# Decays set two units ahead in the matrix memory, and negated maxima with scaled queries in attention

## The chip, the cores and the metric

The kernel runs on one core of a Trainium2 chip. The core has TensorE (PE), VectorE (DVE), ScalarE (ACT), GpSimd (POOL) and SyncE (SP), which issues most transfers. The metric is the device time of one execution in microseconds.

## What is computed

One batch of 256 latent and 256 context tokens of width 1024 goes through two blocks, all in float32. The first block has two layers, each a gated feed-forward part, a mixer of attention with a short convolution, and a second feed-forward part. The second block has a matrix memory ("mlstm") and a gated recurrence ("hgrn") beside each other, forwards and backwards, and a convolutional feed-forward part. The change touches the attention and the matrix memory:

```python
def attend(q, k, v):
    s = jnp.einsum('bqhd,bkhd->bhqk', q, k, preferred_element_type=jnp.float32) * ATTN_SCALE
    p = jax.nn.softmax(s, axis=-1).astype(v.dtype)
    return jnp.einsum('bhqk,bkhd->bqhd', p, v)

def step(carry, inp):                       # matrix memory, chunk by chunk
    C, n, m = carry
    qc, kc, vc, ic, fc = inp
    b = jnp.cumsum(fc, axis=-1)
    dlog = jnp.where(causal, b[..., :, None] - b[..., None, :] + ic[..., None, :], -jnp.inf)
    inter = b + m[..., None]
    mt = jnp.maximum(inter, jnp.max(dlog, axis=-1))
    w_intra = jnp.exp(dlog - mt[..., None])
    w_inter = jnp.exp(inter - mt)
    s = jnp.einsum('bhtd,bhsd->bhts', qc, kc) * w_intra
    num = jnp.einsum('bhts,bhsv->bhtv', s, vc) + w_inter[..., None] * jnp.einsum('bhtd,bhdv->bhtv', qc, C)
    den = jnp.sum(s, axis=-1) + w_inter * jnp.einsum('bhtd,bhd->bht', qc, n)
    h = num / jnp.maximum(jnp.abs(den), jnp.exp(-mt))[..., None]
    ...
```

## The kernel before

Each engine runs a program of its own, written out by hand, and the engines meet at counting semaphores. On each engine the order of work is the order in the code. `own.mark` counts an instruction of the same engine, and `own.wait` or `own.link` lets the engine wait for it. Weights stream from memory in units of 1 MB into a ring of slots (`raw`) that SyncE fills as slots come free. ACT rounds each half unit to a high part (L1094), DVE takes the remainder (L1565), and PE makes three products of high and low parts (L555, L563). That is most of the time.

**Attention.** After the projections ACT copies the queries of 8 heads out of PSUM (L1299) and DVE the keys. Then come units, each one head and 128 query rows: 32 in layer 0 (16 of them over 256 context keys, 16 over all 512 keys), 16 in layer 1 (512 keys). For unit n PE makes the scores (L852), DVE the row maximum (L1925, `small`) and its product with the negative scale (L1927), ACT the exponential with that as bias and the scale as factor, and its row sum (L1319), DVE the reciprocal (L1933) and the scaling (L1934). PE transposes the probabilities (L861) for unit n-2 of its loop, ACT copies them (L1328), PE multiplies them with the values for pairs of units (L874), and DVE splits the result into `h_hi` and `h_lo` (L1942, L1943). L1949 is a remainder of the convolution beside it. Three banks hold scores and two the transposes, so that three units are under way.

**Matrix memory.** It is computed in closed form, not chunk by chunk. There are 8 units: unit n is head n // 2 in direction d = n % 2. For each head PE makes the scores of 512 keys and 256 queries (`scores`, L997). For each unit PE spreads the row of running maxima over the partitions into bank 2 + d (`maxima`, L989). DVE adds the causal mask on two blocks (`mask`, L2145). ACT takes the exponentials, three with a bias from the bank (L1444) and two of the masked blocks (L1447); together they are `ml_decay[d]`. DVE weighs scores with them (`weigh`, L2158 and L2162), PE multiplies by the values (L1022), and `num_out` makes the rows: DVE the denominator and its reciprocal (L2186 to L2188), then for even units a scaled copy on ACT (L1474), for odd ones an addition on DVE (L2193) and sums of squares on ACT (L1482). Between these stand pieces of the other recurrence's output: a gate on DVE (`gated`, L2208), its rounding on ACT (`high`, L1489) and the remainder on DVE (`out_rest`, L2239). There are two buffers of decays and of weights, one for each direction. PE's loop over n waits for the weighing of unit n, then makes the maxima of unit n+2, then (odd n) the scores of the next head, then the products of unit n. ACT's loop takes the exponentials of unit n and then the rows of unit n-1. In the trace all these tiles are called `arena`, the PSUM banks `bank`, the maxima's operands `x` and `consts`, the causal mask `late`.

Of the kernel before, what the change touches and what calls it, by code (L numbers as in the profile page):

```python
# [27 lines left out]
ACT = mybir.ActivationFunctionType  # L28
ALU = mybir.AluOpType
AX_X = mybir.AxisListType.X  # L30
# [151 lines left out]
def build_program(nc, stream, columns_in, cond_in, x_in, ctx2_in, params_in, consts_in, out, until=None):  # L182
    with ExitStack() as stack:
# [326 lines left out]
        def _(pe):  # L510
# [455 lines left out]
            def mlstm():  # L966
# [43 lines left out]
                for n in range(2 * MH):  # L1010
                    hd, d = n // 2, n % 2
                    pe.wait_ge(sem("ml_weighted"), n + 1)
                    if n + 2 < 2 * MH:
                        maxima(n + 2)
                    if d == 1 and hd + 1 < MH:
                        scores(hd + 1)
# [64 lines left out]
        def _(act):  # L1081
# [191 lines left out]
            def mla_and_conv(i):  # L1273
# [21 lines left out]
                for n in list(range(0, 16, 2)) + list(range(16, 20)):  # L1295
                    act.wait_ge(sem(f"head_sum{tag}"), n + 1)
                    acc = bank[IN_BANK[8 + n % 4]]
                    if n < 16:
                        nc.scalar.activation(q_heads[0:QK, n // 2, t0:], acc[0:QK, 0:T - t0], ACT.Copy)\  # L1299
                            .then_inc(sem(f"query_moved{tag}"), 1)  # L1300
                    else:
                        nc.scalar.activation(values[:, n - 16, :], acc[:, :], ACT.Copy).then_inc(sem(f"query_moved{tag}"), 1)
# [5 lines left out]
                for n in range(len(units) + 2):  # L1308
# [5 lines left out]
                    if n < len(units):  # L1314
                        keys = units[n][2]
                        act.wait_ge(sem(f"negmax{tag}"), n + 1)
                        if n >= 3:
                            act.wait_ge(sem(f"prob_turned{tag}"), n - 2)
                        nc.scalar.activation(probs[:, n % 3, 0:keys], bank[SCORE_BANKS[n % 3]][:, 0:keys], ACT.Exp,  # L1319
                                             bias=small[:, n % 4:n % 4 + 1], scale=SCALE,  # L1320
# [113 lines left out]
            def mlstm():  # L1434
                act.wait_ge(sem("u_cols"), 1)
                nc.scalar.activation(small[:, 40:56], small[:, 40:56], ACT.Exp).then_inc(sem("ml_floor"), 1)
                for n in range(2 * MH):
# [4 lines left out]
                    for c, a, b in ((0, 0, LAT), (1, 0, LAT), open_chunk):  # L1442
                        u = u_cols[:, MH * (4 * d + c) + hd:MH * (4 * d + c) + hd + 1]
                        nc.scalar.activation(ml_decay[d][:, c, a:b], bank[2 + d][:, a:b], ACT.Exp, bias=u, scale=-1.0)  # L1444
# [6 lines left out]
                    last.then_inc(sem("ml_decayed"), 1)  # L1451
                    if n >= 1:
                        num_out(n - 1)
                    if 2 <= n < 2 + MH:
                        high("hg", n - 2)
# [98 lines left out]
        def _(dve):  # L1554
# [296 lines left out]
            def mla_and_conv(i):  # L1851
# [69 lines left out]
                for n in range(len(units) + 3):  # L1921
                    if n < len(units):
                        keys = units[n][2]
                        dve.wait_ge(sem(f"score{tag}"), n + 1)
                        own.link(nc.vector.tensor_reduce(small[:, 24 + n % 4:25 + n % 4], bank[SCORE_BANKS[n % 3]][:, 0:keys],  # L1925
                                                         axis=AX_X, op=ALU.max))
                        nc.vector.tensor_scalar(small[:, n % 4:n % 4 + 1], small[:, 24 + n % 4:25 + n % 4], -SCALE, None, ALU.mult)\  # L1927
                            .then_inc(sem(f"negmax{tag}"), 1)
# [204 lines left out]
            def mlstm():  # L2133
# [5 lines left out]
                def mask(n):  # L2139

                    hd, d = n // 2, n % 2
                    dve.wait_ge(sem("ml_max"), n + 1)
                    for c in range(2):
# [386 lines left out]
```

## Time and profile before

| | us |
|---|---|
| median of 3 runs | 2290.14 |
| lowest and highest | 2286.48, 2291.62 |
| the profiled execution | 2290.66 |
| its span in the trace | 2288.9 |

| engine | busy us | share of the span |
|---|---|---|
| TensorE, products | 2172.6 | 95% |
| TensorE, weight loads | 1814.5 | 79% |
| VectorE | 1518.6 | 66% |
| ScalarE | 860.6 | 38% |
| GpSimd | 133.5 | 6% |

The trace lists every instruction with start, length, line and the tiles it writes and reads. A busy share over the whole span mixes stages with different limits. The stages that the change touches are the attention of layer 0 (about 536 to 598 us), that of layer 1 (about 1460 to 1499 us) and the matrix memory (about 1969 to 2023 us). The granted clock is the share of TensorE's 2.4 GHz that was granted in a stretch: 1.00 is 2.4 GHz, 0.50 is 1.2 GHz.

### The profile page before, as it was taken

How to read it: one execution, taken by the hardware profiler on the slowest of the kernel's cores; microseconds unless marked ns; L12 is line 12 of the kernel's file. 1: busy time of each engine (PE TensorE's matmuls, PEld its weight loads, DVE VectorE, ACT ScalarE, POOL GpSimd, SP SyncE). 2: the span in 40 equal slices, each digit the busy share in tenths (PEclk: the TensorE clock that was granted, in tenths of full speed). 3: DMA queues.
4: the chain of work that ended last, by engine and by line, in shares of the span. 5: the costliest groups of instructions: out<-in, count | busy, mean ns of one | idle time of the engine just before them, and what ended most of it. 6: DMA issues, size and time to landing. Idle time of an engine off the chain costs nothing.

```text
span 2288.9 us, 29162 instructions
## 1 busy us (share of the span) xinstructions
PE 2172.6 (95%) x11516; PEld 1814.5 (79%) x11516; DVE 1518.6 (66%) x2645; ACT 860.6 (38%) x1439; POOL 133.5 (6%) x104
## 2 busy tenths in 40 slices
PE   5999999998999999999999999989997998879998
PEld 3888888874688888888888888589996887778888
DVE  2777777747677775666575557676545767458984
ACT  3432322424452222243323235454444356432233
POOL 1000000024000000000000000310011000010001
PEclk8999999999999999999999999999997999879999
DMA  6455554320135556535455633236553232024444
GB/s 254 175 189 198 196 189 175 138 92 19 56 121 192 185 203 201 206 108 175 166 201 194 211 140 121 70 133 225 182 198 104 92 111 74 1 90 150 147 147 147
DMA packets 61415, 342.11 MB, mean 149 GB/s; under 512 B 6624, under 2 KB 8672, under 8 KB 31584
## 3 DMA queue, kind: packets, MB, share of 16 engines
q1 hardware_dynamic: 60096, 338.56, 42.4%
q8 instruction: 91, 1.49, 0.3%
q10 hardware_dynamic: 1184, 1.70, 0.2%
q14 instruction: 44, 0.36, 0.0%
HBM read 339.19 MB, written 1.05 MB: 149 GB/s over the span
## 4 chain that ended last, share of the span: by engine, by line
PE 87%; DVE 7%; ACT 2%; issue 2%; DMA 1%; POOL 0%; SPq 0%; DVEq 0%; ACTq 0%; POOLq 0%
PE bank L555 45%; PE bank L563 22%; PE bank L1044 7%; PE bank L629 3%; PE bank L640 1%; DVE w_lo L1565 1%; DMA raw<-stream 1%; PE bank L874 1%; PE bank L832 1%; PE bank L852 1%; DVE arena L2010 1%; ACT w_hi L1094 1%; PE bank L829 1%; DVE arena L2092 1%; DVE small L1925 1%
## 5 line engine op out<-in xcount | busy, mean ns | idle before, releaser
L1565 DVE TENSOR_TENSOR w_lo<-raw,w_hi 128x1024 fp32r<-128x1024 f32 (+1 forms) x389 | 469.2, 1206 | 510.4 <-ACT w_hi L1094 508.9
L1094 ACT ACTIVATE w_hi<-raw 128x1024 fp32r<-128x1024 f32 (+1 forms) x389 | 403.5, 1037 | 1018.9 <-PE bank L555 1010.2
L555 PE MATMUL bank<-hidden_hi,w_hi 128*128 128x512 f32 (+1 forms) x1392 | 492.2, 363 | 2.5 <-ACT w_hi L1094 2.5
L555 PE MATMUL bank<-hidden_lo,w_hi 128*128 128x512 f32 (+1 forms) x1392 | 492.1, 363 | 0.0
L555 PE MATMUL bank<-h_hi,w_hi 128*128 128x512 f32 (+1 forms) x1416 | 460.9, 343 | 6.2 <-ACT w_hi L1094 4.7
L555 PE MATMUL bank<-h_lo,w_hi 128*128 128x512 f32 (+1 forms) x1416 | 458.6, 341 | 0.0
L1598 DVE CUSTOM_DVE_ANT_0 scratch<-columns_raw,late,params 128x1024 f32<-128x1024 f32 x288 | 360.2, 1280 | 6.2 <-issue 5.3
L563 PE MATMUL bank<-hidden_hi,w_lo 128*128 128x512 f32 (+1 forms) x1392 | 308.4, 363 | 2.0 <-DVE w_lo L1565 2.0
L555 PEld LDWEIGHTS bank<-h_hi,w_hi 128*128 128x128 f32 x1416 | 269.2, 190 | 38.2 <-ACT w_hi L1094 4.0
L555 PEld LDWEIGHTS bank<-hidden_hi,w_hi 128*128 128x128 f32 x1392 | 263.5, 189 | 43.8 <-issue 2.9
L555 PEld LDWEIGHTS bank<-hidden_lo,w_hi 128*128 128x128 f32 x1392 | 263.5, 189 | 40.4
L555 PEld LDWEIGHTS bank<-h_lo,w_hi 128*128 128x128 f32 x1416 | 269.2, 190 | 30.3 <-issue 0.5
L563 PE MATMUL bank<-h_hi,w_lo 128*128 128x512 f32 (+1 forms) x1416 | 284.2, 341 | 5.2 <-DVE w_lo L1565 5.2
L563 PEld LDWEIGHTS bank<-hidden_hi,w_lo 128*128 128x128 f32 x1392 | 241.5, 189 | 42.7 <-DVE w_lo L1565 2.2
L563 PEld LDWEIGHTS bank<-h_hi,w_lo 128*128 128x128 f32 x1416 | 228.2, 190 | 35.9 <-DVE w_lo L1565 6.0
L1044 PE MATMUL bank<-h,raw 128*128 128x256 f32 x704 | 153.9, 382 | 1.3 <-DVE h L1726 1.3
L1044 PEld LDWEIGHTS bank<-h,raw 128*128 128x128 f32 x704 | 134.9, 192 | 20.6 <-issue 2.0
L2252 DVE SCALAR_TENSOR_TENSOR arena<-arena,params 128x189 f32<-128x189 f32 (+2 forms) x352 | 122.8, 429 | 20.3 <-ACT arena L1501 20.3
L2328 POOL TENSOR_TENSOR rinv<-squares 128x512 f32<-128x512 f32 (+1 forms) x10 | 13.8, 1380 | 1712.3 <-ACT squares L1116 1712.3
L2328 POOL TENSOR_TENSOR rinv<-rinv,squares 128x512 f32<-128x512 f32 (+1 forms) x40 | 55.6, 1389 | 236.9 <-ACT squares L1116 235.8
L1499 ACT ACTIVATE arena<-bank 128x256 f32<-128x256 f32 x44 | 16.9, 384 | 114.9 <-PE bank L1044 114.9
L1637 DVE SCALAR_TENSOR_TENSOR hidden_lo<-x,scales,hidden_hi 128x256 fp32r<-128x256 f32 x56 | 33.7, 636 | 33.7 <-ACT hidden_hi L1125 33.7
(271 smaller groups left out, 2040.6 us busy)
## 6 DMA issues: line engine op xcount, KB each, us to landing
raw<-stream SPq DMA_DIRECT2D x229, 1024.0 KB, 5.0
columns_raw<-columns_in SPq DMA_DIRECT2D x176, 512.0 KB, 3.8
x<-x_in SPq DMA_DIRECT2D x1, 2048.0 KB, 10.1
late<-cond_in SPq DMA_DIRECT2D x2, 1024.0 KB, 5.9
x<-ctx_in ACTq DMA_DIRECT2D x1, 1024.0 KB, 5.7
out<-x SPq DMA_DIRECT2D x2, 512.0 KB, 3.0
late<-consts_in ACTq DMA_DIRECT2D x1, 640.0 KB, 4.0
consts<-consts_in SPq DMA_DIRECT2D x1, 464.5 KB, 4.3
```

The lines of the kernel that those rows point to most:

```text
L555: last = nc.tensor.matmul(acc, w_hi[:, buffer, kc, :], v(first_chunk + kc), start=start and kc == n == 0, stop=False)
L563: last = nc.tensor.matmul(acc, w_lo[:, buffer, kc, :], hi(first_chunk + kc), start=False, stop=stop and kc == chunks - 1)
L629: last = nc.tensor.matmul(accs[sub], w_hi[:, buffer, kc, :], v(kc), start=kc == m == 0, stop=False)
L640: last = nc.tensor.matmul(accs[sub], w_lo[:, buffer, kc, :], hi(kc), start=False, stop=kc == KC - 1)
L829: last = nc.tensor.matmul(acc[0:NOPE, :], w_kv[:, hd, 0:NOPE], latent[:, 2, :], start=True, stop=True)
L1044: last = nc.tensor.matmul(bank[PAIR_BANKS[j][gv]][:, 0:LAT], raw[at % RING][:, kc, gv * P:(gv + 1) * P], h[:, kc, CTX:], start=kc == 0, st ...
L1094: nc.scalar.activation(w_hi[:, buffer, 0:chunks, :], raw[at % RING][:, 0:chunks, sub * P:(sub + 1) * P], ACT.Copy)\
L1565: nc.vector.tensor_tensor(w_lo[:, buffer, 0:chunks, :], raw[at % RING][:, 0:chunks, sub * P:(sub + 1) * P], w_hi[:, buffer, 0:chunks, :].b ...
L1598: nc.vector.tensor_tensor_reduce(column_products[at % 2], columns_raw[n % COLUMN_RING][:, :], cond_rows[:, c, :], 1.0, bias, ALU.mult, ALU ...
L1637: nc.vector.scalar_tensor_tensor(lo, x[:, kc, a:b], scales[:, kc, which:which + 1], hi.bitcast(F32), ALU.mult, ALU.subtract)\
L2252: nc.vector.scalar_tensor_tensor(acc[:, ro, co], source[:, ri, ci], w, acc[:, ro, co], ALU.mult, ALU.add)\
L2328: nc.gpsimd.tensor_tensor(square_sum[:, t0:], first, squares[:, kc % 4, t0:], ALU.add).then_inc(sem("square_added"), 1)
```

## The change

In attention the reduction itself gives the negative maximum, and the instruction that negated and scaled it is gone. The scale goes into the copy of the queries, and the exponential has no factor any more.

In the matrix memory PE makes the maxima of unit n+2 before it waits for the weighing of unit n. The buffer `ml_decay[d]` is protected by a new wait on DVE ahead of the mask. ACT takes the exponentials of units 0 and 1 ahead of the loop, and in the loop those of unit n+2 ahead of the rows of unit n-1. The roundings of the other recurrence move up by one step on ACT.

```diff
@@ PE, mlstm @@
                 for n in range(2 * MH):
                     hd, d = n // 2, n % 2
-                    pe.wait_ge(sem("ml_weighted"), n + 1)
                     if n + 2 < 2 * MH:
                         maxima(n + 2)
+                    pe.wait_ge(sem("ml_weighted"), n + 1)
                     if d == 1 and hd + 1 < MH:
                         scores(hd + 1)
@@ ACT, mla_and_conv @@
-                        nc.scalar.activation(q_heads[0:QK, n // 2, t0:], acc[0:QK, 0:T - t0], ACT.Copy)\
+                        nc.scalar.activation(q_heads[0:QK, n // 2, t0:], acc[0:QK, 0:T - t0], ACT.Copy, scale=SCALE)\
                             .then_inc(sem(f"query_moved{tag}"), 1)
...
                         nc.scalar.activation(probs[:, n % 3, 0:keys], bank[SCORE_BANKS[n % 3]][:, 0:keys], ACT.Exp,
-                                             bias=small[:, n % 4:n % 4 + 1], scale=SCALE,
+                                             bias=small[:, n % 4:n % 4 + 1],
@@ ACT, mlstm @@
-                for n in range(2 * MH):
+                def decays(n):
+
                     hd, d = n // 2, n % 2
                     act.wait_ge(sem("ml_masked"), n + 1)
...
-                        nc.scalar.activation(ml_decay[d][:, c, a:b], bank[2 + d][:, a:b], ACT.Exp, bias=u, scale=-1.0)
+                        own.mark(nc.scalar.activation(ml_decay[d][:, c, a:b], bank[2 + d][:, a:b], ACT.Exp, bias=u, scale=-1.0))
...
                     last.then_inc(sem("ml_decayed"), 1)
+
+                decays(0)
+                decays(1)
+                for n in range(2 * MH):
+                    if n + 2 < 2 * MH:
+                        decays(n + 2)
                     if n >= 1:
                         num_out(n - 1)
-                    if 2 <= n < 2 + MH:
-                        high("hg", n - 2)
+                    if 1 <= n < 1 + MH:
+                        high("hg", n - 1)
@@ DVE, mla_and_conv @@
-                        own.link(nc.vector.tensor_reduce(small[:, 24 + n % 4:25 + n % 4], bank[SCORE_BANKS[n % 3]][:, 0:keys],
-                                                         axis=AX_X, op=ALU.max))
-                        nc.vector.tensor_scalar(small[:, n % 4:n % 4 + 1], small[:, 24 + n % 4:25 + n % 4], -SCALE, None, ALU.mult)\
-                            .then_inc(sem(f"negmax{tag}"), 1)
+                        nc.vector.tensor_reduce(small[:, n % 4:n % 4 + 1], bank[SCORE_BANKS[n % 3]][:, 0:keys],
+                                                axis=AX_X, op=ALU.max, negate=True).then_inc(sem(f"negmax{tag}"), 1)
@@ DVE, mlstm, mask @@
                     dve.wait_ge(sem("ml_max"), n + 1)
+                    if n >= 2:
+                        dve.wait_ge(sem("ml_weighted"), n - 1)
```

The order on PE in the matrix memory, before, from the maxima of unit 4 (L989 are maxima, L997 scores, L1022 products with the values):

```order
L989 MATMUL bank<-x,consts 128x256 [waits ml_decayed,ml_weighted]
L1022 MATMUL bank<-arena 128x129 [waits ml_moved0]
L1022 MATMUL bank<-arena 128x129 x6
L989 MATMUL bank<-x,consts 128x256 [waits ml_decayed,ml_weighted]
L997 MATMUL bank<-arena 128x256 [waits ml_weighted]
```

The same rows of the changed kernel:

```order
L989 MATMUL bank<-x,consts 128x256 [waits ml_decayed]
L1022 MATMUL bank<-arena 128x129 [waits ml_moved0,ml_weighted]
L1022 MATMUL bank<-arena 128x129 x6
L989 MATMUL bank<-x,consts 128x256 [waits ml_decayed]
L997 MATMUL bank<-arena 128x256 [waits ml_weighted]
```

The order is the same; the wait for the weighing has moved from the maxima to the products behind them.

The order on ACT, before, from the end of the exponentials of unit 1 to the start of those of unit 3:

```order
L1447 ACTIVATE arena<-arena 128x128 x2
L1474 ACTIVATE arena<-bank,small 128x128 [waits ml_rec,scalar_own]
L1474 ACTIVATE arena<-bank,small 128x128
L1444 ACTIVATE arena<-bank,small 128x256 [waits ml_masked,scalar_own]
L1444 ACTIVATE arena<-bank,small 128x256
L1444 ACTIVATE arena<-bank,small 128x128
L1447 ACTIVATE arena<-arena 128x128 x2
L1482 ACTIVATE squares,small<-arena 128x128 [waits ml_moved1,scalar_own]
L1482 ACTIVATE squares,small<-arena 128x128
L1489 ACTIVATE h_hi<-arena 128x256 [waits hg_gated]
L1444 ACTIVATE arena<-bank,small 128x256 [waits ml_masked]
```

The changed kernel from the same place (its L1445, L1448, L1481 and L1496 are the L1444, L1447, L1474 and L1489 of before):

```order
L1448 ACTIVATE arena<-arena 128x128 x2
L1445 ACTIVATE arena<-bank,small 128x256 [waits ml_masked,scalar_own]
L1445 ACTIVATE arena<-bank,small 128x256
L1445 ACTIVATE arena<-bank,small 128x128
L1448 ACTIVATE arena<-arena 128x128 x2
L1445 ACTIVATE arena<-bank,small 128x256 [waits ml_masked,scalar_own]
L1445 ACTIVATE arena<-bank,small 128x256
L1445 ACTIVATE arena<-bank,small 128x128
L1448 ACTIVATE arena<-arena 128x128 x2
L1481 ACTIVATE arena<-bank,small 128x128 [waits ml_rec,scalar_own]
L1481 ACTIVATE arena<-bank,small 128x128
L1496 ACTIVATE h_hi<-arena 128x256 [waits hg_gated,scalar_own]
```

The exponentials of units 2 and 3 now both stand ahead of the scaled copy of unit 0.

## Rows read from the trace of the kernel before

**Rows 1.** The page, part 4: the chain that ended last, by engine.
```profile
PE 87%; DVE 7%; ACT 2%; issue 2%; DMA 1%; POOL 0%; SPq 0%; DVEq 0%; ACTq 0%; POOLq 0%
```

**Rows 2.** Windows: start and end, length, busy time by engine, granted clock, DMA share, GB/s.
```profile
537.00:600.00 63.00, 52.85 (x352) 31.48 (x353) 49.05 (x166) 36.42 (x101) 4.57 (x4) 0.97 0.00 1
1969.00:2022.00 53.00, 37.32 (x169) 29.49 (x169) 25.80 (x91) 20.21 (x73) 0.00 (x0) 0.73 0.00 1
```

**Rows 3.** The chain in order of time, both attentions: start, length; first and last of L1927.
```profile
536.99 0.16 DVE small L1927
...
1493.18 0.17 DVE small L1927
```

**Rows 4.** Timeline, layer 1, one turn: start, length, engine, line [idle before <-releaser].
```profile
1474.78 0.69 DVE L1925 TENSOR_REDUCE small<-bank 128x1 f32<-128x512 f32 x1 [0.43 <-PE bank L852]
...
1475.51 0.15 DVE L1927 TENSOR_SCALAR small<-small 128x1 f32<-128x1 f32 x1
1475.58 0.15 DVE L1933 RECIPROCAL small<-small 128x1 f32<-128x1 f32 x1
1475.70 0.69 ACT L1319 ACTIVATE arena<-bank,small 128x512 f32<-128x512 f32 x1 [1.47 <-DVE small L1927]
1475.77 0.48 DVE L1934 TENSOR_SCALAR arena<-arena,small 128x512 f32<-128x512 f32 x1
1476.17 0.42 DVE L1949 TENSOR_TENSOR h_lo<-squares,h_hi 128x256 fp32r<-128x256 f32 x1
...
1476.31 0.66 PE L861 MATMUL bank<-consts,arena 128*128 128x128 f32 x4 [0.26 <-DVE arena L1934]
```

**Rows 5.** Timeline, matrix memory, from weighing unit 2 to weighing unit 3.
```profile
1984.22 0.69 DVE L2158 SCALAR_TENSOR_TENSOR arena<-bank,arena 128x512 f32<-128x512 f32 x1 [2.20 <-ACT arena L1447]
...
1985.49 0.69 PE L989 MATMUL bank<-x,consts 4*128 4x256 f32 x2 [1.56 <-DVE arena L2162]
...
1986.30 0.61 DVE L2145 SCALAR_TENSOR_TENSOR arena<-late,small,bank 128x128 f32<-128x128 f32 x2 [0.87 <-PE bank L989]
1986.83 0.48 DVE L2208 SCALAR_TENSOR_TENSOR arena<-bank,params,arena 128x256 f32<-128x256 f32 x1
1987.22 0.15 DVE L2186 SCALAR_TENSOR_TENSOR small<-bank,small 128x2 f32<-128x2 f32 x1
...
1987.80 0.61 DVE L2193 SCALAR_TENSOR_TENSOR arena<-bank,small,arena 128x128 f32<-128x128 f32 x2
...
1989.41 1.07 ACT L1444 ACTIVATE arena<-bank,small 128x256 f32<-128x256 f32 x3
...
1991.08 0.69 DVE L2158 SCALAR_TENSOR_TENSOR arena<-bank,arena 128x512 f32<-128x512 f32 x1 [2.67 <-ACT arena L1447]
```

**Rows 6.** Timeline, matrix memory: scores, maxima, products at either clock; the last rows.
```profile
1977.38 1.64 PEld L1022 LDWEIGHTS bank<-arena 128*128 128x128 f32 x14 [0.33 <-issue]
...
1980.37 1.99 PE L997 MATMUL bank<-arena 128*128 128x256 f32 x8
...
1981.99 1.75 PEld L1022 LDWEIGHTS bank<-arena 128*128 128x128 f32 x14
...
1992.36 1.22 PE L989 MATMUL bank<-x,consts 4*128 4x256 f32 x2 [3.53 <-DVE arena L2162]
...
1993.50 3.76 PE L997 MATMUL bank<-arena 128*128 128x256 f32 x8
1993.69 0.61 DVE L2145 SCALAR_TENSOR_TENSOR arena<-late,small,bank 128x128 f32<-128x128 f32 x2 [1.39 <-PE bank L989]
...
1996.65 1.98 PEld L1022 LDWEIGHTS bank<-arena 128*128 128x128 f32 x14
...
2016.93 2.50 PEld L1022 LDWEIGHTS bank<-arena 128*128 128x128 f32 x14 [3.46 <-DVE arena L2162]
...
2019.76 0.16 DVE L2186 SCALAR_TENSOR_TENSOR small<-bank,small 128x2 f32<-128x2 f32 x1 [2.42 <-PE bank L1022]
```

**Rows 7.** Windows, as rows 2, of the stretch behind the gap of 1.56 us.
```profile
1987.00:1990.00 3.00, 1.83 (x9) 1.53 (x8) 1.31 (x6) 1.50 (x7) 0.00 (x0) 0.50 0.00 0
```

## The prediction

> **What bounds the kernel now.** I read the chain of work that ended last first: 87% of it is TensorE, 7% VectorE, 2% ScalarE [rows 1]. Most of this kernel is a stream of weight products, which the change does not touch. So the change can only matter in its two kinds of stage, and each has to be read alone.
>
> The windows come next. In the attention of layer 0 TensorE is busy 52.85 of 63 us, in the matrix memory 37.32 of 53 us at a mean granted clock of 0.73; the DMA share is 0.00 in both [rows 2]. No transfer runs there, so the ring of weight slots is full, and time taken out of either stage moves all that follows forward without a transfer being late. The attention of layer 1 looks the same with half the units.
>
> In attention the chain goes through the line that negates the maximum (L1927) in almost every pair of units: 23 pieces, of which [rows 3] show the first and the last, 16 in layer 0 and 7 in layer 1. In the matrix memory one pass over a unit goes DVE, PE, DVE, ACT, DVE with no two of them working at once for long [rows 5]: the products weighed (L2158, L2162), then the maxima of the unit two ahead on PE (L989), then its mask on DVE (L2145), then the rows of the unit before (L2186 to L2193), their squares on ACT (L1482), only then the exponentials of the next unit (L1444, L1447), and only then the next weighing.
>
> **Attention, part by part.** (a) *The negation goes.* [rows 4] is one turn of the steady pattern. The reduction starts at 1474.78 and is done at 1475.47; the negation starts at 1475.51; the exponential that needs it starts at 1475.70. ACT starts about 0.04 us after what it waits for, so with the reduction itself giving the negative the exponential starts at 1475.51: 0.19 earlier. On the DVE side the reciprocal starts at 1475.58 and the scaling at 1475.77, 0.99 after the reduction's start. Without a wait between them the reciprocal, which needs nothing of the reduction, starts some 0.09 before the reduction is done, as L1949 does behind L1934 (1475.77 + 0.49 against 1476.17), thus 0.60 after its start; the scaling follows 0.19 later: 0.79 in place of 0.99. Both branches lose about 0.19, so it does not matter which of them the chain takes. What is late next is PE itself: it stood idle 0.26 before the transposes of this turn, more than 0.19, so the whole 0.19 is gained. 23 x 0.19 = **4.4 us**.
>
> The Trainium skill speaks against half of this ("VectorE: DVE Perf Modes", The DRAIN you can't avoid): the next operation does not start before the pipeline has emptied, and a semaphore between two costs nothing extra. By that rule the reciprocal would start at 0.69 and the scaling at 0.91, only 0.08 earlier, and the DVE branch, a few hundredths behind the ACT branch, would hold nearly every turn: 23 x 0.08 = 1.8 us. The trace disagrees with it: the 0.09 us of overlap between L1934 and L1949 in [rows 4].
>
> (b) *A negated reduction.* No row shows one. It reads the same elements, so it cannot be shorter; the nearest row is the plain one, 0.69, so I take nothing. The far end is a second pass, another 0.69 each. (c) *The scale moves* from 48 exponentials to the 16 query copies on ACT, as an immediate factor. L1444 carries a factor and bias, and three of them take 1.07 [rows 5], so I take nothing; were a copy 0.1 longer, 16 of them would be 1.6 us, the upper end.
>
> **Matrix memory, part by part.** Three edits belong together. PE no longer waits for the weighing of unit n before the maxima of unit n+2; VectorE gets that wait ahead of the mask instead, where it stands behind its own weighing anyway (a few hundredths, no one else queued). ACT does the exponentials of unit n+2 ahead of the rows of unit n-1, so they are ready a unit early.
>
> The turn of before [rows 5]: 1984.22 to 1991.08 is 6.86 us for one unit, of which 0.81 is PE's maxima with DVE waiting, and 3.86 (1987.22 to 1991.08) the string of rows, squares and exponentials. After the change the exponentials leave the chain: the set of unit n starts with its mask, long ahead of its weighing.
>
> What is left is a cycle of one head (two units), which I add up at full clock from starts in [rows 5] and [rows 6]: scores, to the next weight load, 1.62 (1980.37 to 1981.99); output products of the odd unit 1.64 (their loads); maxima to mask 0.81 (1985.49 to 1986.30), since they stand behind those products on PE; mask 0.53; another DVE tile operation of 256 columns (gate or remainder) 0.39; rows of the odd unit 1.12 (1987.22 to the end of L2193 at 1988.41, less an overlap of about 0.08); weighing 1.27 (1984.22 to 1985.49). Sum 7.38. The next scores need that weighing, so the cycle closes. The last piece, from the scores of head 3 to the last rows, is 1.62 + 1.85 + 1.12 + 0.39 + 1.27 + 1.85 = 8.10, with 1.85 for output products as far as DVE sees them (1.64 of loads plus 0.2; an estimate). From the scores of head 1 to the last rows: 2 x 7.38 + 8.10 = **22.9 us**. Before, the same stretch is 1980.37 to 2019.76 = **39.4 us**. The maxima ahead of the scores of head 1 also leave their way, some 0.6. Gain 39.4 + 0.6 - 22.9 = **17.1 us**.
>
> That is with the clock up. In the cycle PE works about 6.2 of 7.4 us (1.62 + 2 x 1.64 + 2 x 0.62), and its longest gap is about 1.2 us (mask to scores). Before, the clock went to 1.2 GHz near 1987 (granted 0.50 after it, [rows 7]) behind a gap of 1.56 us [rows 5] and again behind longer ones. In attention PE has about the same share of work, and gaps of 0.3 to 0.5, and its clock stays at 2.4 GHz but for one short stretch at the start. So I take the high clock.
>
> The cost on ACT: the scaled copy of an even unit now stands behind 1.5 us of exponentials. PE's products two units on and VectorE's rows of the odd unit wait for it. In the cycle above it is done some 1.9 us before VectorE asks, so nothing is added.
>
> **Sum.** The profiled execution took 2290.66 us (span 2288.9 and 1.8 around it), 0.5 above the median. 2290.66 - 4.4 - 17.1 = **2269.2 us**.
>
> **Rivals.**
> *The clock stays low in the matrix memory* (0.18). Against it is the even load; for it that the old gap of 1.56 is not far above the new 1.2, and that the maxima use only four rows of the array. Then from [rows 5] and [rows 6]: scores 3.15, output products 2.50 (2.83 as seen by DVE), maxima to mask 1.33, the rest as above: 3.15 + 2.50 + 1.33 + 0.53 + 0.39 + 1.12 + 1.27 = 10.29, twice, and 3.15 + 2.83 + 1.12 + 0.39 + 1.27 + 2.83 = 11.59: 32.2. Gain 39.4 + 0.6 - 32.2 = 7.8, and the time 2290.66 - 4.4 - 7.8 = 2278.5. Falls in a part of it give times between.
> *VectorE does not start the reciprocal before the reduction is done* (0.10). Then the scaling starts at 0.69 + 0.03 + 0.19 = 0.91 in place of 0.99, and attention gives 23 x 0.08 = 1.8: 2271.8. For it: behind L1925 no row shows an operation without a wait. Against it: L1949 behind L1934 [rows 4]. The rule of the Trainium skill named above says this.
> *The copies queued on ACT take the place of the wait removed* (0.08): if the 1.9 us of slack is not there, up to 1.5 us for each of three heads comes back, 4.5: 2273.7.
> *Slower: the negated reduction is dear* (0.02). Each of the 23 places then costs its extra time e in place of the gain, 23 x (e - 0.19), against 17.1. It decides from e = 0.93, a reduction of 1.6 in place of 0.69; with three times the plain one (e = 1.38) the time is 2290.66 + 27.4 - 17.1 = 2301. Nothing speaks for it but that no row shows one.
> *The edits do nothing* (0.02): should the chain in both stages run beside what they cut, the time stays at 2290. The rows of the chain in [rows 3] and the idle of DVE and ACT in [rows 5] speak against it.
>
> **How the numbers follow.** The forecast case has 0.60, from 2265 (the clock then also stays up into the final transposes and the first output products, some 2.4 us, and attention gives a little more) to 2273. The range reaches over the other clock case and its 1.6 us of dearer copies: 2264 to 2280. About 0.2% (4.6 us) is what a measurement of this kernel can tell from no change. Faster by more than that 0.94, within it 0.03 (edits without effect, and part of the dear reduction), slower 0.03.
>
> **What would show it.** Right: L1927's counterpart gone, and a turn of two units in layer 1 at 4.22 in place of 4.42 us; exponentials 0.73 after the start of their reduction in place of 0.92; scaling at 0.79. In the matrix memory, scores 7.4 us apart, granted clock near 1.00 over the stage in place of 0.73, no wait of a weighing for exponentials, and a stage of about 36 us in place of 53. Wrong: scores more than 10 us apart at a clock of 0.50, a weighing or rows of an odd unit waiting on ACT's scaled copy, a reduction well over 0.69, or scalings still 0.9 behind their reduction. If transfers after the stages end later against PE than now, the gain would be lost there, which the empty queue denies.

## The result, and the profile after

The changed kernel takes **2269.07 us**, the median of 4 runs (2264.03 to 2271.17); the kernel before, measured beside it, takes 2290.88 us, the median of 4 (2286.48 to 2292.72). The ratio is **0.9904**, with a 95% interval of 0.9882 to 0.9927: 21.8 us faster. The profiled execution took 2267.79 us, 2266.0 of it span, 22.9 us of span less than the profiled one of before.

First the windows of the changed kernel over the whole matrix memory, and inside it. The columns are start and end, length, busy time of PE, PE's loads, DVE, ACT and POOL with their counts, granted clock, DMA share and GB/s.

```profile
1963.00:1967.00 4.00, 3.51 (x11) 2.38 (x11) 2.33 (x10) 2.58 (x8) 0.00 (x0) 0.64 0.01 2
1967.00:1971.00 4.00, 4.00 (x15) 3.12 (x14) 2.73 (x9) 1.27 (x5) 0.00 (x0) 0.51 0.02 4
1971.00:1974.00 3.00, 3.00 (x19) 2.18 (x19) 2.13 (x6) 1.49 (x5) 0.00 (x0) 1.00 0.00 0
...
1963.70:1997.40 33.70, 30.20 (x168) 24.56 (x168) 24.10 (x85) 18.28 (x67) 0.00 (x0) 0.90 0.00 1
```

The stage, from the first maxima to the last rows' denominator, is 33.6 us long; the same stretch of before is 50.2. PE has the same number of instructions (168 here, 169 in the slightly wider window of [rows 2]), and its granted clock is 0.90 in place of 0.74 over the same stretch (0.73 in the window of [rows 2]). All of the low clock (1.2 GHz) lies in the first 7 us, before the scores of head 1. From 1971 on the clock is 2.4 GHz to the end.

Next the timeline of the changed kernel, from the scores of head 2 to those of head 3, where [rows 5] has before's turn, of one head earlier. The columns are start, length, engine, line, and in brackets the idle time before and what ended it. L2165 and L2169 weigh, L2152 masks, L2193 and L2200 are the rows (before: L2186 and L2193), L1445 is the exponentials and L1481 the scaled copy of the even unit.

```profile
1981.58 1.97 PE L997 MATMUL bank<-arena 128*128 128x256 f32 x8 [1.10 <-DVE arena L2169]
...
1983.17 1.75 PEld L1022 LDWEIGHTS bank<-arena 128*128 128x128 f32 x14
...
1983.38 1.73 PE L1022 MATMUL bank<-arena 128*128 128x129 f32 x14
1983.58 0.69 DVE L2165 SCALAR_TENSOR_TENSOR arena<-bank,arena 128x512 f32<-128x512 f32 x1 [0.22 <-PE bank L997]
1983.59 0.63 ACT L1481 ACTIVATE arena<-bank,small 128x128 f32<-128x128 f32 x2
...
1985.04 0.69 PE L989 MATMUL bank<-x,consts 4*128 4x256 f32 x2
...
1985.66 1.83 PE L1022 MATMUL bank<-arena 128*128 128x129 f32 x14
1985.83 0.61 DVE L2152 SCALAR_TENSOR_TENSOR arena<-late,small,bank 128x128 f32<-128x128 f32 x2 [1.03 <-PE bank L989]
1986.36 0.15 DVE L2193 SCALAR_TENSOR_TENSOR small<-bank,small 128x2 f32<-128x2 f32 x1
1986.47 1.10 ACT L1445 ACTIVATE arena<-bank,small 128x256 f32<-128x256 f32 x3 [1.95 <-DVE arena L2152]
...
1986.94 0.61 DVE L2200 SCALAR_TENSOR_TENSOR arena<-bank,small,arena 128x128 f32<-128x128 f32 x2
1987.46 0.42 DVE L2246 TENSOR_TENSOR h_lo<-arena,h_hi 128x256 fp32r<-128x256 f32 x1
1987.80 0.69 DVE L2165 SCALAR_TENSOR_TENSOR arena<-bank,arena 128x512 f32<-128x512 f32 x1
...
1989.16 1.97 PE L997 MATMUL bank<-arena 128*128 128x256 f32 x8 [1.04 <-DVE arena L2169]
```

No weighing waits for ACT any more: L2165 at 1983.58 waits 0.22 us, for PE, and at 1987.80 for nothing, where L2158 in [rows 5] waited 2.20 and 2.67 us for L1447. The exponentials run in ACT's own idle time (1.95 us before L1445, which waits for the mask). The scores of one head and the next are 7.58 us apart; in before they were 13.13 (1980.37 to 1993.50, [rows 6]).

Third, the timeline of one turn in the attention of layer 1, the counterpart of [rows 4].

```profile
1469.91 0.69 DVE L1932 TENSOR_REDUCE small<-bank 128x1 f32<-128x512 f32 x1 [0.43 <-PE bank L852]
...
1470.52 0.15 DVE L1938 RECIPROCAL small<-small 128x1 f32<-128x1 f32 x1
1470.64 0.69 ACT L1319 ACTIVATE arena<-bank,small 128x512 f32<-128x512 f32 x1 [1.36 <-DVE small L1932]
1470.71 0.49 DVE L1939 TENSOR_SCALAR arena<-arena,small 128x512 f32<-128x512 f32 x1
...
1474.15 0.69 DVE L1932 TENSOR_REDUCE small<-bank 128x1 f32<-128x512 f32 x1 [0.43 <-PE bank L852]
```

The negation (L1927) is gone. The exponential starts 0.73 us after its reduction starts, where it was 0.92; the scaling starts at 0.80, where it was 0.99. The reciprocal starts 0.61 after the start of a reduction of 0.69, so it begins before the reduction is done. The negated reduction takes 0.69 us, exactly as the plain one. A turn of two units is 4.23 or 4.24 us (1469.91 to 1474.15 is one), where it was 4.42.

**Where the 22.9 us of span went.** I cut both profiled executions at the same landmarks: start-up (to the first L664) gave 4.3 us, attention of layer 0 0.3, the stretch between the attentions lost 1.5, attention of layer 1 gave 2.6, the matrix memory 16.6, the tail 0.5. The sum is 22.9, but only the matrix memory can be read from this pair alone. The start-up is unchanged code. On its chain a landing took 7.15 us in the trace of before (from 29.07) and 5.35 in that of the changed kernel (from 29.75), and the same 16 matmuls (L629) took 6.71 us from 42.06 and 3.88 from 40.54. Over twelve traces of this study the start-up lasted from 51.7 to 59.5 us. The two attentions are blurred by a short stretch of low clock whose place and length differ from trace to trace. These are windows of before, then of the changed kernel, with the columns above:

```profile
1392.00:1398.00 6.00, 4.01 (x30) 3.61 (x28) 5.22 (x13) 2.75 (x5) 0.00 (x0) 1.00 0.53 178
...
1464.00:1470.00 6.00, 6.00 (x30) 3.42 (x29) 4.28 (x13) 4.10 (x10) 0.00 (x0) 0.72 0.01 3
```
```profile
1392.00:1398.00 6.00, 4.64 (x26) 4.64 (x27) 3.36 (x5) 2.63 (x4) 0.00 (x0) 0.72 0.14 60
...
1464.00:1470.00 6.00, 5.88 (x45) 3.41 (x42) 4.01 (x12) 3.80 (x10) 0.00 (x0) 1.00 0.00 0
```

Before had its low stretch inside the attention of layer 1 (0.72 at 1464), the changed kernel some 70 us ahead of it (0.72 at 1392). The filler kernel below, with before's attention and its low stretch also near 1392, splits it: about 1.1 of the 2.6 us gained in layer 1 is that stretch having left, and the 1.5 us lost between the attentions is there in that kernel too. Whether the place of this stretch is chance is not shown. It stands between 1460 and 1470 in all four traces with before's attention and no fillers (layer 1 takes 38.0 us in each), and between 1392 and 1402 in all seven with the changed attention (35.4 or 35.5 us) and in that of the filler kernel. What attention really gave must come from runs with that change alone.

### The profile page after: what moved, and what is told of

Its sections match the earlier page's. It is cut to its first block, busy times and chain, and to the rows that moved or that the text cites. A ratio compares the mean times of both kernels' runs of the same rounds, so it can differ in the third digit from the quotient of the medians.

```text
span 2266.0 us, 29113 instructions
## 1 busy us (share of the span) xinstructions
PE 2163.8 (95%) x11516; PEld 1808.0 (80%) x11516; DVE 1512.1 (67%) x2597; ACT 860.4 (38%) x1439; POOL 133.4 (6%) x104
## 4 chain that ended last, share of the span: by engine, by line
PE 88%; DVE 7%; ACT 2%; issue 1%; DMA 1%; POOL 0%; SPq 0%; DVEq 0%; ACTq 0%; POOLq 0%
PE bank L555 45%; PE bank L563 23%; PE bank L1044 7%; PE bank L629 3%; PE bank L640 1%; DVE w_lo L1572 1%; PE bank L852 1%; DMA raw<-stream 1%; PE bank L874 1%; PE bank L832 1%; DVE arena L2015 1%; ACT w_hi L1094 1%; PE bank L829 1%; DVE arena L2097 1%; DVE small L1932 1%
## 5 line engine op out<-in xcount | busy, mean ns | idle before, releaser
L1644 DVE SCALAR_TENSOR_TENSOR hidden_lo<-x,scales,hidden_hi 128x256 fp32r<-128x256 f32 x56 | 33.7, 636 | 33.5 <-ACT hidden_hi L1125 33.5
```

The source lines that it names most:

```text
L1644: nc.vector.scalar_tensor_tensor(lo, x[:, kc, a:b], scales[:, kc, which:which + 1], hi.bitcast(F32), ALU.mult, ALU.subtract)\
```

## The experiments

My theory: the two stages give 4.4 and 17.1 us, and they add; in the matrix memory the exponentials leaving the chain are the cause, and the better clock follows from that. The rivals: the clock itself is the cause; the reciprocal waits for the end of the reduction; ACT's queue has little room.

**The changed kernel again**, unchanged.

> The changed kernel once more, for a second trace of its stages and a narrower interval. Theory: matrix memory, from its first maxima to its last rows, 33.6 us as in the first trace (50.2 before), a turn of two units in the attention of layer 1 4.23 us (4.42 before), time 2269 plus or minus 3 us, ratio 0.990. Rival: the start of the kernel, which the change does not touch, ended 4.3 us earlier in the first trace of the changed kernel than in that of before; if that were part of the change's doing it would stand here too, if it is chance it would not.

It took 2267.94 us (4 runs), against 2291.06 (15 runs): 0.9904, 0.9891 to 0.9918. In its trace the matrix memory is 33.5 us (33.6 before). The attention of layer 0, however, is 59.2 us, against 61.8 in the first trace of the very same kernel. So this stage, read from one pair of traces, carries an error of over 2 us, and the matrix memory of about 0.1.

**The attention edits alone**, on the kernel before (all three):

```
-nc.scalar.activation(q_heads..., acc..., ACT.Copy)
+nc.scalar.activation(q_heads..., acc..., ACT.Copy, scale=SCALE)
-                     bias=small[:, n % 4:n % 4 + 1], scale=SCALE,
+                     bias=small[:, n % 4:n % 4 + 1],
-own.link(nc.vector.tensor_reduce(small[:, 24 + n % 4:25 + n % 4], ..., op=ALU.max))
-nc.vector.tensor_scalar(small[:, n % 4:n % 4 + 1], small[:, 24 + n % 4:25 + n % 4], -SCALE, None, ALU.mult)
+nc.vector.tensor_reduce(small[:, n % 4:n % 4 + 1], ..., op=ALU.max, negate=True)
```

> Only the attention part: negated reduction, scale in the query copies. Theory A (both branches of a turn lose 0.19 us, 23 turns): 4.4 us faster than before, 2286.5, turns of 4.23 us in layer 1, matrix memory 50 us as before. Theory B (VectorE does not start the reciprocal before the reduction is done): 1.8 us faster, turns of 4.34 us. Theory C: the shares of the two attentions that run at 1.2 GHz differ from run to run by more than this gain, so that the whole time shows 0 to 6 us while the turns show 0.19 each.

2286.15 us (11 runs) against 2291.06: 0.9982, 0.9973 to 0.9991. That is 4.1 us, between 2.1 and 6.2. The rival's 1.8 lies just outside; 4.4 is well within. The timeline of layer 1 in this kernel shows which of the two holds:

```profile
1473.88 0.69 DVE L1925 TENSOR_REDUCE small<-bank 128x1 f32<-128x512 f32 x1 [0.43 <-PE bank L852]
...
1478.11 0.69 DVE L1925 TENSOR_REDUCE small<-bank 128x1 f32<-128x512 f32 x1 [0.43 <-PE bank L852]
```

The turn is 4.23 us, as in the full change, where the rival had 4.34; the matrix memory is 50.15 us, as before.

**The matrix memory alone**: the changed kernel with those three edits taken back.

```
-nc.vector.tensor_reduce(small[:, n % 4:n % 4 + 1], ..., op=ALU.max, negate=True)
+own.link(nc.vector.tensor_reduce(small[:, 24 + n % 4:25 + n % 4], ..., op=ALU.max))
+nc.vector.tensor_scalar(small[:, n % 4:n % 4 + 1], small[:, 24 + n % 4:25 + n % 4], -SCALE, None, ALU.mult)
...
```

> Only the matrix memory part: maxima ahead of the wait on TensorE, exponentials two units ahead on ScalarE, the wait on VectorE. Theory: 16.6 us faster than before (2274), matrix memory 33.6 us long at a mean clock near 0.9. Rival: without the attention part the phase of the clock is another and TensorE falls to 1.2 GHz inside the stage: 43 us long, 8 us faster (2283).

2273.4 us (5 runs), 0.9926, 0.9912 to 0.9939: 17.0 us. The stage is 33.65 us, as in the full change. 4.1 and 17.0 make 21.1 of the 22.0 measured for both on the same chip, so the two parts add within what can be measured.

**Exponentials ahead alone.** The matrix memory edits with the wait of PE put back ahead of the maxima; attention as before.

```
                 for n in range(2 * MH):
                     hd, d = n // 2, n % 2
+                    pe.wait_ge(sem("ml_weighted"), n + 1)
                     if n + 2 < 2 * MH:
                         maxima(n + 2)
-                    pe.wait_ge(sem("ml_weighted"), n + 1)
```

> Of the matrix memory part only ScalarE's order (and VectorE's wait): the exponentials two units ahead, but TensorE waits for the weighing of unit n before the maxima of unit n+2, as before. Theory (the exponentials behind the rows were the long piece of the turn, the maxima behind the weighing a short one): the scores of the heads about 8.0 us apart in place of 7.6, the stage 35 to 36 us, so 14 to 15 us faster than before. Rival (the wait of the maxima for the weighing was the long piece): the stage 43 us or more, at most 7 us faster.

2277.22 us (5 runs), 0.9942, 0.9929 to 0.9954: 13.3 us. The stage is 37.0 us in place of 50.2, and its granted clock rises to 0.86. First the window of the stage in this kernel, then its timeline where PE still waits.

```profile
1970.60:2007.70 37.10, 32.00 (x168) 25.86 (x168) 24.11 (x85) 18.31 (x67) 0.00 (x0) 0.86 0.00 1
```
```profile
1988.98 0.69 PE L989 MATMUL bank<-x,consts 4*128 4x256 f32 x2 [1.63 <-DVE arena L2171]
```

The maxima wait 1.63 us for the weighing, and the mask (1989.78) comes 0.80 after their start; the scores are 8.2 us apart. I had expected 8.0, and a stage of 35 to 36 us, one less than it is. The exponentials make 13.2 of the 16.6 us, on ACT alone (with the clock that rises with them).

**Maxima early alone**, on the kernel before: PE's wait behind the maxima, and the wait of VectorE ahead of the mask.

```
-                    pe.wait_ge(sem("ml_weighted"), n + 1)
                     if n + 2 < 2 * MH:
                         maxima(n + 2)
+                    pe.wait_ge(sem("ml_weighted"), n + 1)
...
                     dve.wait_ge(sem("ml_max"), n + 1)
+                    if n >= 2:
+                        dve.wait_ge(sem("ml_weighted"), n - 1)
```

> Of the matrix memory part only TensorE's order and VectorE's wait: the maxima ahead of the wait for the weighing, ScalarE's order as before. Theory (the exponentials behind the rows hold the turn): the scores about 10.9 us apart at 2.4 GHz and 12.5 at 1.2 GHz, the stage 43 to 49 us, so 2 to 7 us faster than before. Rival (the maxima were the long piece): 34 to 37 us, 13 or more faster.

2285.51 us (8 runs) against 2289.7 (13 runs): 0.998, 0.997 to 0.999, so 4.6 us; the stage is 47.6 us, 2.6 less than before (the rest of the 4.6 is within the interval of 2.3 either way). The timeline of this kernel shows why it is so little:

```profile
1982.58 0.61 DVE L2195 SCALAR_TENSOR_TENSOR arena<-bank,small,arena 128x128 f32<-128x128 f32 x2
...
1983.28 0.31 ACT L1482 ACTIVATE squares<-arena 128x128 f32<-128x128 f32 x1 [3.66 <-DVE arena L2195]
...
1985.86 0.69 DVE L2160 SCALAR_TENSOR_TENSOR arena<-bank,arena 128x512 f32<-128x512 f32 x1 [2.67 <-ACT arena L1447]
```

The chain rows, squares, exponentials, weighing is whole: 3.28 us, with ACT idle for 3.66 ahead of it. The mask is ready early and lies there. Alone the two edits make 2.6 + 13.2 = 15.8 of the 16.6 us; they all but add, since they shorten two different links in series.

**Is it the clock?** The kernel before, with matmuls in PE's gaps whose results nobody reads. They fill the waits for the weighing and change no order of the others.

```
+            FILL = (0, 0, 2, 6, 0, 6, 0, 5)
...
+                    if FILL[n]:
+                        pe.wait_ge(sem(f"ml_moved{d}"), hd)
+                        for _ in range(FILL[n]):
+                            nc.tensor.matmul(bank[4 + d][:, 0:LAT], k_ml[:, hd, 0:P], q_ml[:, hd, :], start=True, stop=True, ...)
                     pe.wait_ge(sem("ml_weighted"), n + 1)
```

> The kernel before with filler products on TensorE (2, 6, 6 and 5 of 256 columns before the maxima steps of units 2, 3, 5 and 7, into a bank that is overwritten afterwards), which fill its gaps and keep its clock up; the results do not use them. Theory (the gain of the matrix memory is the order; the low clock is a consequence of the gaps and costs 3 to 4 us of the 16.6): the stage 46 to 48 us at a clock of 0.85 or more. Rival (most of the gain is the clock): the stage near 38 us or less.

2285.02 us (6 runs), 0.9976, 0.9964 to 0.9988: 5.5 us. The window of its stage, and then the scores of heads 1 and 2 in its timeline:

```profile
1967.00:2015.00 48.00, 40.68 (x206) 32.59 (x206) 24.62 (x87) 18.42 (x67) 0.00 (x0) 0.90 0.00 1
```
```profile
1977.85 1.99 PE L999 MATMUL bank<-arena 128*128 128x256 f32 x8
...
1990.46 1.99 PE L999 MATMUL bank<-arena 128*128 128x256 f32 x8
```

The granted clock over the stage is 0.90, just what the changed kernel has, up from 0.74; the stage is 47.5 us, 2.7 shorter, and the tail behind it is 1.2 us shorter too (267.9 against 269.1). The fillers are not quite clean: once they hold the maxima up by some 0.3 us, and in the next head the clock falls for some 3.5 us. But between the two scores shown the clock is 1.00 throughout, and they are 12.61 us apart, against 13.13 in before and 7.6 in the changed kernel. So in the order of before, the clock is worth some 3 us of 50 in this stage, and not 16. The low clock of before was for the most part a consequence of the gaps, which cost what they cost at either level.

**Does the overlap of reciprocal and reduction matter?** The changed kernel with a wait of VectorE for its own reduction.

```
                         nc.vector.tensor_reduce(..., negate=True).then_inc(sem(f"negmax{tag}"), 1)
+                        dve.wait_ge(sem(f"negmax{tag}"), n + 1)
```

> The changed kernel with VectorE waiting for its own negated reduction before the reciprocal, so that the two cannot overlap. Theory A (without a wait the next operation starts some 0.09 us before the one in front is done): the scaling 0.90 us after the start of its reduction in place of 0.79, turns of two units in layer 1 about 4.33 us in place of 4.23, over both attentions 1.5 to 2.5 us slower than the changed kernel. Theory B (the pipeline empties anyway, a wait costs nothing): no row moves, turns of 4.23.

2270.34 us (4 runs), 0.9907, 0.9892 to 0.9922: not to be told from the 0.9904 without it. The timeline of its turn in layer 1:

```profile
1469.98 0.69 DVE L1932 TENSOR_REDUCE small<-bank 128x1 f32<-128x512 f32 x1 [0.43 <-PE bank L852]
...
1470.71 0.16 DVE L1939 RECIPROCAL small<-small 128x1 f32<-128x1 f32 x1
...
1470.91 0.49 DVE L1940 TENSOR_SCALAR arena<-arena,small 128x512 f32<-128x512 f32 x1
...
1471.45 0.66 PE L861 MATMUL bank<-consts,arena 128*128 128x128 f32 x4 [0.20 <-DVE arena L1940]
1472.04 1.09 PE L874 MATMUL bank<-arena 128*64 128x128 f32 x16
...
1474.22 0.69 DVE L1932 TENSOR_REDUCE small<-bank 128x1 f32<-128x512 f32 x1 [0.43 <-PE bank L852]
```

The wait costs 0.13 us where it stands (scaling 0.93 after the start of the reduction, against 0.80), and PE's transposes (L861) start 0.13 later too, 1.47 after the reduction's start (1.34 without the wait). But the attended products (L874) start 2.06 after the reduction's start, and 2.05 without the wait (1471.96 in the changed kernel), because they wait for ACT's copy (L1328), which stands behind the exponential; the turn is 4.24 us either way. In layer 1 the scaling had room, and the exponential's branch holds the turn. In layer 0 the wait costs something: that stage is 62.4 us, against 61.8 in the changed kernel's trace with as long a stretch of low clock. I expected turns of 4.33 and 1.5 to 2.5 us in all; neither theory had that.

**Room in ACT's queue.** The changed kernel with copies of a constant into a scratch tile ahead of the scaled copy of each even unit, 3 of them (shown) and, in a second kernel, 15.

```
                     if d == 0:
+                        for _ in range(3):
+                            own.link(nc.scalar.activation(junk[2 * hd], const("ident", 0, P), ACT.Copy))
```

> The changed kernel with 3 copies of 128x128 (about 0.3 us each, into a tile that is overwritten later) on ScalarE ahead of every even unit's scaled copy, which so comes about 0.9 us later. Theory (in the changed kernel that copy is done some 2.7 us before VectorE asks for it): the matrix memory stays at 33.5 us, scores 7.6 us apart. Rival (the queue on ScalarE is as tight as the wait it replaced): about 0.9 us more for each of the heads, 36 us.

> The same with 15 copies, about 4.5 us later. Theory: the slack of 2.7 us is used up and the rest, 1.8 us or somewhat less, comes back for each of the three later heads: 37 to 39 us, scores about 9.4 us apart, with VectorE or TensorE waiting for the scaled copy in the rows. Rival (ScalarE has room for it all): 33.5 us.

Each kernel ran once, with the kernel before at 2286.37 us beside both. With three copies it took 2266.67, and in its timeline they take 1.00 us, the scaled copy is done at 1984.25 and the rows ask for it at 1985.93. The last line is TensorE's, one head later:

```profile
1982.59 1.00 ACT L1480 ACTIVATE squares<-consts 128x128 f32<-128x128 f32 x3
...
1983.62 0.63 ACT L1483 ACTIVATE arena<-bank,small 128x128 f32<-128x128 f32 x2
...
1985.93 0.61 DVE L2202 SCALAR_TENSOR_TENSOR arena<-bank,small,arena 128x128 f32<-128x128 f32 x2
...
1991.97 1.80 PE L1022 MATMUL bank<-arena 128*128 128x129 f32 x14 [0.29 <-ACT arena L1483]
```

The stage is 33.7 us, as without them, though one group of products now waits 0.29 us for the copy. With fifteen it took 2283.36, and the stage is 48.8 us, 15.2 longer; scores are 12.5 and 12.1 us apart. The waits of that kernel (total, times, longest), and then its timeline:

```profile
PE bank L1022 <- ACT arena L1483: 10.1, 3, 4.6
```
```profile
1987.18 5.11 ACT L1480 ACTIVATE squares<-consts 128x128 f32<-128x128 f32 x15
...
1993.10 3.26 PE L1022 MATMUL bank<-arena 128*128 128x129 f32 x14 [1.60 <-ACT arena L1483]
```

I expected the part beyond the slack alone, a stage of 37 to 39 us. The copies stand ahead of all four even units. Three of the four sets run inside the stage, and of their 15.3 us 15.2 came back; the fourth ends behind it, where the tail is 2.0 us longer.

I had taken the slack at the wrong engine. The scaled copy reads a bank that TensorE's products of the next even unit overwrite, so TensorE waits for it too, and it asks before VectorE does: in the changed kernel the copy is done at 1984.22 and those products start at 1985.66, 1.44 us later (1.27 one head earlier, 0.72 one head later), where VectorE's rows start at 1986.94. The three waits of L1022, 10.1 us, are at TensorE. As an estimate from these rows, three times 5.1 less 3.4 of room is 11.9 us of waiting. The other 3.3 us go with the clock, which is 0.72 over the stage: the products behind the wait take 3.26 us in place of 1.83. No run separates the two.

**A better order?** The changed kernel with the weighing of an odd unit on VectorE taken ahead of the rows of the unit two earlier, so that the scores wait for less. PE's maxima run one unit further ahead.

```
+                maxima(2)
                 for n in range(2 * MH):
...
-                    if n + 2 < 2 * MH:
-                        maxima(n + 2)
                     pe.wait_ge(sem("ml_weighted"), n + 1)
                     if d == 1 and hd + 1 < MH:
                         scores(hd + 1)
+                    if n + 3 < 2 * MH:
+                        maxima(n + 3)
...
-                    weigh(n)
+                    if n % 2 == 0 or n < 3:
+                        weigh(n)
...
+                    if n >= 2 and n % 2 == 0:
+                        weigh(n + 1)
```

> The changed kernel with two more moves in the matrix memory: TensorE makes the maxima of unit n+3 before the products of unit n (and those of unit 2 ahead of the loop), and VectorE weighs an odd unit before it makes the rows of the unit two earlier. Theory (in the changed kernel a head costs 7.6 us, of which VectorE waits 1.0 for the maxima and has 1.1 of rows ahead of the weighing that the next scores wait for; TensorE's own work is 6.2): scores about 6.3 us apart, the stage 30 to 31 us in place of 33.6, 3 us faster than the changed kernel. Rival: the order shifts the waits elsewhere (the copies on ScalarE, the products' banks) and the stage stays at 33 us.

2266.73 us (4 runs), 0.9894, 0.9877 to 0.991. By its time alone it can't be told from the changed kernel, but its trace (one) shows a stage of 31.15 us, 2.5 shorter, where I had expected 30 to 31, and the stage of the changed kernel repeated within 0.15 in three traces. In its timeline:

```profile
1978.42 1.89 PE L997 MATMUL bank<-arena 128*128 128x256 f32 x8
...
1982.84 0.69 DVE L2166 SCALAR_TENSOR_TENSOR arena<-bank,arena 128x512 f32<-128x512 f32 x1 [0.52 <-PE bank L1023]
...
1984.55 0.61 DVE L2201 SCALAR_TENSOR_TENSOR arena<-bank,small,arena 128x128 f32<-128x128 f32 x2
1984.91 1.46 PE L997 MATMUL bank<-arena 128*128 128x256 f32 x6
```

The weighing (L2166) stands ahead of the rows (L2201), the scores no longer wait (no bracket), and come every 6.5 us in place of 7.6. PE is busy for 30.0 of the stage's 31.1 us there, so little more can be had from order alone.

## Why the prediction was right

The forecast was 2269.2 us, the time 2269.07. So close a hit owes something to chance, since a timed median here moves by a microsecond or two: both parts were put in too high (4.4 for 4.1, 17.1 for 16.6 to 17.0), and the difference of the two medians, 21.8, came out above the 21.1 that the parts make. The steps, one by one:

**The stage to look at, and no transfer late: right.** The stretches behind the stages kept their length (from attention to the matrix memory 470.71 and 470.68 us; the tail 269.1 and 268.6).

**Attention, 4.4 us: right in sign and size.** Measured alone, 4.1 (2.1 to 6.2). The exponential at 0.73 and the scaling at 0.80 came as forecast (0.73, 0.79), the turn at 4.23 (4.22). Against the filler kernel, whose attention is that of before and had no low clock in layer 1 (36.94 us), the changed one takes 35.44: 1.5 us, or 8 x 0.19. In layer 0 traces with equally long low clock can be compared: 62.1 and 59.2 us where it lasts about 3.5 us, 64.1 and 61.8 where it lasts about 10.5. They are 2.9 and 2.3 apart, where 16 x 0.19 is 3.0. One reason in this step was idle in layer 1: that both branches had to lose 0.19. The linked reduction gave back 0.13 of the DVE branch and the turn stayed, so only the exponential's branch counted there.

**A negated reduction and the moved scale for nothing: right.** 0.69 us as before, and the 16 query copies (L1299) take 379 to 596 ns with a median of 486, where they took 379 to 595 with the same median.

**Matrix memory, 17.1 us: right in mechanism, 0.5 us too high.** The sum from the scores of head 1 was 22.9 us and is 23.4: 7.64 + 7.58 + 8.20. The mis-sized terms can be read in the second group of rows above. From scores to maxima PE takes 3.46 us (1981.58 to 1985.04), where 1.62 + 1.64 = 3.26 stood. The loads of the odd unit take 1.75 us, not 1.64: [rows 6] has 1.75 at 1981.99, right behind the scores, and I took the 1.64 of another group. And 0.12 pass between the end of the loads (1984.92) and the maxima, which the sum left out. From weighing to scores it is 1.36 (1987.80 to 1989.16), not 1.27. Maxima to mask 0.79, mask 0.53, rows 1.10 and remainder 0.34 are within 0.05 of what was put in. The 0.6 us ahead of the scores of head 1 came as forecast (10.8 became 10.2).

**The clock: half right.** It does stay high through all of the cycle. "Near 1.00 over the stage" was wrong, 0.90, since I forgot the beginning: head 0, its maxima, scores and transposes run at 1.2 GHz in both kernels (0.67 in before from 1974 to 1978). As it is there in both, it did not move the gain.

**The copy's slack on ACT: right in sign, at the wrong engine.** 1.9 us was put in, up to where VectorE asks. The copy is done at 1984.22 and VectorE's rows start at 1986.94, 2.7 later, but TensorE's products need it first, at 1985.66. The prediction names this wait and gives it no price. The room is 1.44 us there, and 0.72 in the last head; the change stayed within it.

**The rivals.** The low clock in the matrix memory did not come; its sum had output products at 2.50 us, where they take 3.26 to 3.35 at 1.2 GHz in the kernel with fifteen copies. The reciprocal does start early, by 0.08 us (0.61 after the start of a reduction of 0.69). The overlap of L1949 on which the prediction rests is 0.08 by [rows 4] (1475.77 + 0.48 against 1476.17), not 0.09. The prediction gives the rule of the Trainium skill ("VectorE: DVE Perf Modes", The DRAIN you can't avoid) without its exception: the same paragraph says that a next operation that is not held starts earlier. With that sentence the trace agrees. With the section's other statement, that a semaphore between two operations costs nothing extra (measured there on a row of copies), it does not: here the wait costs 0.13 us. This rival was priced wrong as well: it would have kept 0.11 from the turn at 23 places, 2.5 us, but with just such a wait layer 1 stayed within 0.1 us and layer 0 lost some 0.7. The copies queued on ACT need over 1.4 us more at TensorE before they count, 0.7 in the last head. The negated reduction is not dear.

**Open** is how the 15.2 us of the fifteen copies divide exactly between wait and clock, and why the low clock comes near 1392 us in eight traces and near 1464 in four.

## What to carry to other kernels

When two engines hand a tile back and forth, write down the cycle from the trace, start to start, and ask of each link whether it needs the one in front or merely stands behind it in its engine's queue: here the exponentials only stood behind rows and squares, and moving them up two units was worth 13 of 50 us without one instruction less. A low clock in a stage full of gaps is first of all a sign of the gaps; filling them with idle matmuls gave 2.7 us, closing them 16.6. To price the room of an item in a queue, look up every engine that waits for it; the first to ask sets the room, and here it was not the one I had looked at. And do not read a stage from one pair of traces where the clock wanders: repeat the kernel, and take each edit alone.

## What was new about the hardware

- VectorE starts an operation without a wait 0.08 to 0.09 us before the one in front of it, a reduction of 0.69 us, is done; with a wait for that reduction it starts 0.04 after its end (1470.71 against 1470.67).
- Unchanged code differs from trace to trace: the start-up of 55 us by 7.8 us (51.7 to 59.5), the first attention of the changed kernel by 2.6 us (61.8 and 59.2), with a clock of 0.50 in three windows of 3 us in the longer one and in one in the shorter; the windows of both, the longer first:

```profile
534.00:537.00 3.00, 2.73 (x8) 1.82 (x8) 2.17 (x7) 1.53 (x6) 2.84 (x3) 0.50 0.00 0
537.00:540.00 3.00, 3.00 (x13) 1.54 (x12) 2.22 (x6) 1.19 (x4) 0.45 (x1) 0.50 0.00 0
540.00:543.00 3.00, 3.00 (x6) 1.18 (x5) 1.33 (x4) 0.81 (x3) 0.00 (x0) 0.50 0.00 0
```
```profile
537.00:540.00 3.00, 3.00 (x8) 1.50 (x6) 2.17 (x5) 1.68 (x6) 2.72 (x3) 0.50 0.00 0
540.00:543.00 3.00, 3.00 (x17) 1.47 (x16) 2.40 (x8) 1.11 (x4) 0.00 (x0) 1.00 0.00 0
```

- Work of 5.1 us put three times into a queue with 3.4 us of room in all cost 15.2 us, not the 11.9 beyond the room; the clock was 0.72 in place of 0.90, and output products behind a wait took 3.26 us in place of 1.83.
